# A depthwise convolution moved from diagonal matrices and VectorE onto quarter-width matmuls over shifted copies

## The chip, the cores and the metric

The kernel runs on one core of a Trainium2 chip. The core has TensorE (matmuls, PE in the profile), VectorE (DVE), ScalarE (ACT), GpSimd (POOL) and SyncE (SP), and 16 DMA engines that all queues share. The metric is device time in microseconds (us) for one execution, smaller is better.

## What is computed

The reference is a two-layer transformer for 256 positions of width 1024, in f32. Layer 0 is differential attention and a dense feed-forward part. Layer 1 is a conformer convolution and a mixture of 8 experts with 2 chosen for each position. Each layer ends with a gated embedding. The change touches the convolution of layer 1 and the start of the second expert job:

```python
def conformer_conv(h, w_pw1, b_pw1, w_dw, b_dw, ln_g, ln_b, w_pw2, b_pw2):
    u = h @ w_pw1 + b_pw1
    a, g = jnp.split(u, 2, axis=-1)
    u = a * jax.nn.sigmoid(g)
    u = lax.conv_general_dilated(u, w_dw[:, None, :], window_strides=(1,),
        padding=[(CONV_WIDTH - 1, 0)], feature_group_count=D_MODEL, ...) + b_dw
    u = jax.nn.silu(layer_norm(u, ln_g, ln_b))
    return u @ w_pw2 + b_pw2

def moe_swiglu(h, w_router, b_router, w_gate, w_up, w_down):
    ...
    for e in range(N_EXPERTS):
        out = out + gates[..., e:e + 1] * swiglu(h, w_gate[e], w_up[e], w_down[e])
```

CONV_WIDTH is 31 and the convolution is depthwise: every one of the 1024 channels has 31 taps of its own, and output position s is the sum over k of tap k times input position s - 30 + k.

## The kernel before, in words

**Weights.** SyncE streams all weights through a ring of 14 slots (`weight_ring`), one piece of 1 MB in each slot, in the order in which they are used. A piece holds two units of 128x1024. For a dense unit ScalarE rounds the raw weights to `weight_hi` (L1159), VectorE subtracts to get `weight_lo` (L1614, in the second expert job L2203) and TensorE multiplies three times (L516 to L518); the two have four buffers each. `lo_done` counts the units whose raw data is no longer needed, and SyncE's `load` (L381) waits on it before it refills a slot. Everything on SyncE is in one order, so that whatever it waits for holds back all loads behind it.

**The convolution stage.** `U_PW1` (16 units) is the first projection of the convolution, `U_PW2` (8 units) the second, `U_MOE` the first expert's first unit. The projection puts channels in the partitions, in eight blocks of 128 channels. It makes blocks 0 to 3 first (8 units), then blocks 4 to 7. After each half `glu_scale` (L1893, L1895), the sigmoids on ScalarE (L1382) and `glu` (L1904) leave `conv_in_T`, eight blocks with 30 zeros and then 256 positions. `glu_done` is 1 when blocks 0 to 3 are there and 2 when all are.

- TensorE does blocks 0 to 3 (`PE_BLOCKS`). For each tap ScalarE scales the identity by the 128 channels' tap (L1393, `diagonals`), and TensorE multiplies this diagonal with the shifted input (L785): 31 matmuls of 256 columns in f32 for each block. ScalarE empties the bank and adds the bias (L1401).
- VectorE does blocks 4 to 7 (`DVE_BLOCKS`): for each block one multiplication with bias (L1924) and 30 multiply-adds (L1928).

Then comes the layer norm: a matmul with ones for the mean (L795, eight blocks), centring (L1935), squares (L1417), a matmul with ones for the variance (L799), root, reciprocal, scaling, silu, and the second projection.

**The experts.** VectorE works out a table of jobs. Job 0 is a light one (64 rows or fewer, raw f32 weights, `light_job`, matmuls L866 and L875), job 1 a big one (`big_job`: the expert with most rows, hi/lo matmuls L516 to L518 for 128 rows and quarter-width f32 matmuls for 32 rows more, L1008), then pairs of a light and a small job, then light ones. At the start of `big_job` TensorE waits for `selg_done`, which VectorE raises when the gated one-hot of the job is made (`one_hot_gated`, L2034); on VectorE this comes behind the four additions of job 0's result (`scatter_add`, L2146). The one-hot is first read by the transposes behind the fourth unit (`in_gate`, i == 3).

GpSimd loads two rows that are spread over all partitions: the bias of the second projection once the first scaled pair of the layer norm is there (`cn_done`, L501), which VectorE adds to the residual (L1949), and the norm's gains later (L504).

Of the kernel before, what the change touches and what calls it, by code (L numbers as in the profile page):

```python
# [38 lines left out]
def program(nc, x, p, mix_norm_g, ffn_norm_g, attn_w_qkv, attn_w_o, attn_g_q, attn_g_k,  # L39
# [52 lines left out]
    with ExitStack() as ctx:  # L92
        def sb(name, shape, dt=F32, to=ctx):
            return to.enter_context(nc.sbuf_tensor(name, shape, dt))
# [23 lines left out]
        taps, mask, upper, wr, wr2, lamv = overlay(  # L118
            ("conv_taps", [P, TAPS * KT], F32), ("causal_mask", [P, P], F32), ("strict_upper", [P, P], F32),
            ("router_raw", [P, KT, NE], F32), ("router_hi_lo", [P, KT, 2 * NE], F32R),  # L120
            ("lambda_vectors", [P, 4, HD], F32))
        xel, sgl, hTl, selTl = overlay(
# [36 lines left out]

        cT, cy, csq = overlay(("conv_in_T", [P, KT, TAPS - 1 + S], F32), ("conv_out_T", [P, KT, S], F32),  # L160
                              ("conv_square", [P, KT, S], F32))
# [5 lines left out]
        _, pnat = overlay(("before_p_rows", [P, 5 * D], F32), ("p_rows", [P, T, 2 * P], F32))  # L167
        sb("stage_region", [P, KT * (TAPS - 1 + S) + 2 * KT * S])
        NDIAG = 8

        def diag(n):

            at = CW + n % 4 * P
            return xn[:, n % NDIAG // 4, at:at + P]

# [17 lines left out]
        NV = 91  # L193
        TAPROWS = TAPS * KT // 2
        stage_v = kT[0:NV, 0, 0:P]
        stage_t = [kT[0:TAPROWS, 1, 0:P], kT[0:TAPROWS, 2, 0:P]]

# [65 lines left out]
        glu_done = sem("glu_done")  # L263
        diag_done = sem("diag_done")
        diag_used = sem("diag_used")
        convp_done = sem("convp_done")
        conv_done = sem("conv_done")
        mean_ready = sem("mean_ready")
# [104 lines left out]
        def _(sp):  # L373
# [14 lines left out]
            def feed_forward(first, wg, wu, wd, j=None, proj=None):  # L388
# [44 lines left out]
            tap_rows = conv_w_dw[0].rearrange("k (c n) -> (k c) n", n=P)  # L433
            for i in range(2):
                sp.dma_start(stage_t[i], tap_rows[i * TAPROWS:(i + 1) * TAPROWS, :]).then_inc(consts_in, 16)
            sp.wait_ge(consts_in, 16 * N_CONSTS)
# [73 lines left out]
        def _(pe):  # L510
# [78 lines left out]
            def feed_forward(u0, n0, j, job, side, gap=0):  # L589

                u = u0
                for s in range(STEPS):
# [18 lines left out]
                    for i in range(4):  # L611
# [7 lines left out]

            pe.wait_ge(consts_in, 16 * N_CONSTS)  # L620
            pe.wait_ge(masks_done, 4)
            pe.transpose(ps[:, 0, 0:NV], stage_v, ident[0:NV, 0:NV])
            pe.transpose(ps[:, 0, P:P + TAPROWS], stage_t[0], ident[0:TAPROWS, 0:TAPROWS])
            pe.transpose(ps[:, 0, 2 * P:2 * P + TAPROWS], stage_t[1],
                         ident[0:TAPROWS, 0:TAPROWS]).then_inc(vecsT_ready, 1)

# [152 lines left out]

            n = 0  # L780
            pe.wait_ge(glu_done, 1)
            for ch in PE_BLOCKS:
                for k in range(TAPS):
                    pe.wait_ge(diag_done, n + 1)
                    pe.matmul(ps[:, 4 + ch, 0:S], diag(n), cT[:, ch, k:k + S],  # L785
                              start=k == 0, stop=k == TAPS - 1).then_inc(diag_used, 1)
                    n += 1

            pe.wait_ge(glu_done, 2)
            for n, ch in enumerate(PE_BLOCKS + DVE_BLOCKS):  # L790
                if ch in PE_BLOCKS:
                    pe.wait_ge(convp_done, PE_BLOCKS.index(ch) + 1)
                else:
                    pe.wait_ge(conv_done, DVE_BLOCKS.index(ch) + 1)
                last = pe.matmul(ps[:, 0, 0:S], ones[:, :], cy[:, ch, :], start=n == 0, stop=n == KT - 1)  # L795
            last.then_inc(mean_ready, 1)
# [185 lines left out]
            def big_job(j):  # L982
# [89 lines left out]
                def in_gate(s):  # L1072

                    def behind(i):
# [78 lines left out]
        def _(act):  # L1153
# [231 lines left out]

            def diagonals(first, n):

                for m in range(first, n):
                    i, k = m // TAPS, m % TAPS
                    if m >= NDIAG:  # L1390
                        act.wait_ge(diag_used, m - NDIAG + 1)
                    at = k * KT + PE_BLOCKS[i]
                    act.activation(diag(m), ident[:, :], ACT.Copy, scale=taps[:, at:at + 1]).then_inc(diag_done, 1)  # L1393
                    if i and k == 4:
                        conv_out(i - 1)

            def conv_out(i):

                ch = PE_BLOCKS[i]
                act.wait_ge(diag_used, TAPS * (i + 1))  # L1400
                act.activation(cy[:, ch, :], ps[:, 4 + ch, 0:S], ACT.Identity,  # L1401
                               bias=vecs[:, V_BDW + ch:V_BDW + ch + 1]).then_inc(convp_done, 1)

            split.to(U_PW1 + 7 + 4)
            sigmoids(0)
            diagonals(0, NDIAG)
            split.to(U_PW1 + 15 + 4)
            diagonals(NDIAG, NDIAG + 4)
            sigmoids(1)
            split.to(U_PW2 + 4)  # L1410
            diagonals(NDIAG + 4, TAPS * len(PE_BLOCKS))
            conv_out(len(PE_BLOCKS) - 1)
            act.wait_ge(mean_ready, 1)
# [197 lines left out]
        def _(dve):  # L1611
# [45 lines left out]


            dve.memset(eps, EPS)
            own.step(dve.memset(lneps, LN_EPS))  # L1660
# [7 lines left out]
            for t in range(T):  # L1668
# [3 lines left out]
            dve.tensor_copy(vecs[:, 0:NV], ps[:, 0, 0:NV])  # L1672
            own.step(dve.tensor_copy(taps[:, :].rearrange("p (a n) -> p a n", a=2),
                                     ps[:, 0, P:3 * P].rearrange("p (a n) -> p a n", a=2)[:, :, 0:TAPROWS]))
            own.step(dve.tensor_scalar(gsub, vecs[:, V_GSUB:V_GSUB + 1], 1.0 - LAM0, None, ALU.mult))
# [209 lines left out]
            own.wait(n)  # L1885
            dve.sem_inc(rdiag_done, 1)
            own.step(dve.memset(cT[:, :, 0:TAPS - 1], 0.0))

# [30 lines left out]
            last_of = {}  # L1919
            for k in range(TAPS):  # L1920
                for ch in DVE_BLOCKS:
                    src, w = cT[:, ch, k:k + S], taps[:, k * KT + ch:k * KT + ch + 1]
                    if k == 0:
                        last_of[ch] = own.add(dve.tensor_scalar(  # L1924
                            cy[:, ch, :], src, w, vecs[:, V_BDW + ch:V_BDW + ch + 1], ALU.mult, ALU.add))
                        continue
                    own.wait(last_of[ch])
                    ins = dve.scalar_tensor_tensor(cy[:, ch, :], src, w, cy[:, ch, :], ALU.mult, ALU.add)  # L1928
                    if k < TAPS - 1:
                        last_of[ch] = own.add(ins)  # L1930
                    else:
                        ins.then_inc(conv_done, 1)
            dve.wait_ge(mean_done, 1)
# [394 lines left out]
```

## Time and profile before

| | us |
|---|---|
| median of 3 runs (1554.34 to 1562.11) | 1556.78 |
| the profiled execution, its own time | 1555.64 |
| its span, first to last instruction | 1553.9 |
| TensorE busy in the span | 1447.0 (93%) |
| VectorE busy | 770.5 (50%) |
| ScalarE busy | 665.9 (43%) |
| DMA, mean rate over the span | 285 GB/s |

The span is what the rows of the trace add up to. The profiled execution took 1.74 us more than its span, and the median of the runs lies 1.14 us above it. The busy shares are averages over stages with different limits. An f32 matmul has two records in the trace, so that L785 with 124 matmuls stands there as x248, and L1008 with 32 matmuls in a section as x64; an fp32r matmul (L516 to L518) has one.

### The profile page before, as it was taken

To read this page: it belongs to the slowest core of one execution; us is meant where nothing else is said; L and a number is where in the kernel's file an instruction comes from. 1 tells how busy PE (TensorE), PEld (TensorE's weight loads), DVE (VectorE), ACT (ScalarE), POOL (GpSimd) and SP (SyncE) were. 2 spreads that over 40 slices of the span, in tenths; PEclk is the share of its full clock that TensorE was granted. 3 is DMA by queue.
4 is the path that set the end of the run, shared out by engine and by line. 5 is a ranking of instruction groups with operands and counts; after the bars stand their busy time and mean duration, and the time that the engine had idled before them with its cause. 6 is when DMAs were issued, how large, how long until landed. Compare 5 with 4: busy or idle time off the path is not lost.

```text
span 1553.9 us, 19566 instructions
## 1 busy us (share of the span) xinstructions
PE 1447.0 (93%) x7460; PEld 987.9 (64%) x7460; DVE 770.5 (50%) x1029; ACT 665.9 (43%) x955; POOL 9.1 (1%) x23
## 2 busy tenths in 40 slices
PE   6988999999889977989999999999899999998777
PEld 5866788887789865337777534887335887342236
DVE  5665554455666956025676301988104897000016
ACT  4575544444556742014565201777004775000014
POOL 1000000000000000000000000000000000000000
PEclk9988999999999986998999999999999999999999
DMA  9923555555444022998768699999999999999991
GB/s 312 362 93 104 177 178 189 185 190 189 136 163 136 1 82 75 413 406 351 287 255 324 220 413 406 412 408 410 357 406 412 413 408 410 410 406 412 413 401 63
DMA packets 131334, 442.43 MB, mean 285 GB/s; under 512 B 7059, under 2 KB 7398, under 8 KB 118966
## 3 DMA queue, kind: packets, MB, share of 16 engines
q1 hardware_dynamic: 130144, 438.46, 73.7%
q0 software_dynamic: 928, 2.79, 0.6%
q8 instruction: 58, 0.95, 0.2%
q14 instruction: 22, 0.18, 0.0%
q10 hardware_dynamic: 182, 0.05, 0.0%
HBM read 440.22 MB, written 1.05 MB: 284 GB/s over the span
## 4 chain that ended last, share of the span: by engine, by line
PE 79%; DMA 10%; DVE 4%; ACT 2%; issue 2%; SPq 2%; ACTq 0%; DVEq 0%
PE psum L516 17%; PE psum L518 17%; PE psum L517 17%; PE psum L866 15%; DMA weight_ring<-in_moe_w_down 4%; DMA weight_ring<-in_moe_w_gate 4%; PE psum L785 3%; SPq L381 2%; DMA weight_ring<-in_moe_w_up 2%; PE psum L1008 1%; PE psum L831 1%; PE psum L829 1%; PE psum L1022 1%; DVE weight_lo L1614 1%; PE psum L541 1%
## 5 line engine op out<-in xcount | busy, mean ns | idle before, releaser
L1159 ACT ACTIVATE weight_hi<-weight_ring 128x1024 fp32r<-128x1024 f32 x412 | 431.0, 1059 | 257.8 <-PE psum L518 252.9
L1614 DVE TENSOR_TENSOR weight_lo<-weight_ring,weight_hi 128x1024 fp32r<-128x1024 f32 x328 | 393.9, 1223 | 176.5 <-ACT weight_hi L1159 170.8
L866 PE MATMUL psum<-weight_ring,silu_gate 128*64 128x512 f32 x960 | 219.8, 608 | 13.3 <-DMA weight_ring<-in_moe_w_up 5.6
L516 PE MATMUL psum<-weight_hi,act_hi 128*128 128x512 f32 x448 | 180.2, 402 | 11.6 <-issue 5.6
L517 PE MATMUL psum<-weight_lo,act_hi 128*128 128x512 f32 x448 | 178.3, 398 | 0.0
L518 PE MATMUL psum<-weight_hi,act_lo 128*128 128x512 f32 x448 | 178.1, 398 | 0.0
L2159 DVE TENSOR_TENSOR hidden<-silu_gate,psum 128x512 f32<-128x512 f32 (+1 forms) x20 | 12.4, 622 | 332.7 <-PE psum L866 296.7
L866 PEld LDWEIGHTS psum<-weight_ring,silu_gate 128*64 128x64 f32 x960 | 67.2, 139 | 153.0 <-issue 130.9
L516 PE MATMUL psum<-weight_hi,job_act_hi 128*128 128x512 f32 x336 | 136.3, 406 | 5.4 <-issue 4.9
L866 PE MATMUL psum<-weight_ring,hidden_T 128*64 128x512 f32 x560 | 128.5, 598 | 12.7 <-DMA weight_ring<-in_moe_w_down 12.6
L517 PE MATMUL psum<-weight_lo,job_act_hi 128*128 128x512 f32 x336 | 133.8, 398 | 0.0
L518 PE MATMUL psum<-weight_hi,job_act_lo 128*128 128x512 f32 x336 | 133.8, 398 | 0.0
L2203 DVE TENSOR_TENSOR weight_lo<-weight_ring,weight_hi 128x1024 fp32r<-128x1024 f32 x84 | 101.8, 1224 | 48.6 <-ACT weight_hi L1159 46.1
L1471 ACT ACTIVATE hidden_T<-psum 128x512 f32<-128x512 f32 (+1 forms) x20 | 10.9, 544 | 244.9 <-PE psum L891 244.9
L516 PE MATMUL psum<-weight_hi,hidden_T_hi 128*128 128x512 f32 x280 | 111.0, 397 | 0.0
L518 PE MATMUL psum<-weight_hi,hidden_T_lo 128*128 128x512 f32 x280 | 110.6, 395 | 0.0
L517 PE MATMUL psum<-weight_lo,hidden_T_hi 128*128 128x512 f32 x280 | 110.6, 395 | 0.0
L516 PEld LDWEIGHTS psum<-weight_hi,act_hi 128*128 128x128 f32 x448 | 85.4, 191 | 32.0 <-issue 10.0
L866 PEld LDWEIGHTS psum<-weight_ring,hidden_T 128*64 128x64 f32 x560 | 37.9, 136 | 95.4 <-issue 66.5
L518 PEld LDWEIGHTS psum<-weight_hi,act_lo 128*128 128x128 f32 x448 | 85.3, 190 | 20.2
L517 PEld LDWEIGHTS psum<-weight_lo,act_hi 128*128 128x128 f32 x448 | 85.5, 191 | 19.3
L516 PEld LDWEIGHTS psum<-weight_hi,job_act_hi 128*128 128x128 f32 x336 | 64.0, 191 | 25.8 <-issue 8.4
(336 smaller groups left out, 1645.8 us busy)
## 6 DMA issues: line engine op xcount, KB each, us to landing
weight_ring<-in_moe_w_gate SPq DMA_DIRECT2D x112, 1024.0 KB, 18.3
weight_ring<-in_moe_w_up SPq DMA_DIRECT2D x112, 1024.0 KB, 18.1
weight_ring<-in_moe_w_down SPq DMA_DIRECT2D x112, 1024.0 KB, 16.0
weight_ring<-in_ffn_w_gate SPq DMA_DIRECT2D x14, 1024.0 KB, 5.2
weight_ring<-in_ffn_w_up SPq DMA_DIRECT2D x14, 1024.0 KB, 5.1
weight_ring<-in_ffn_w_down SPq DMA_DIRECT2D x14, 1024.0 KB, 5.1
weight_ring<-in_attn_w_qkv SPq DMA_DIRECT2D x12, 1024.0 KB, 14.3
weight_ring<-in_conv_w_pw SPq DMA_DIRECT2D x12, 1024.0 KB, 5.1
```

Of the source, the lines that this page charges most:

```text
L381: sp.dma_start(dst, src).then_inc(piece_in[slot], 16)
L516: pe.matmul(dst, ahi_, bhi_, start=first, stop=False, **kw)
L517: pe.matmul(dst, ahi_, blo_, start=False, stop=False, **kw)
L518: return pe.matmul(dst, alo_, bhi_, start=False, stop=last, **kw)
L541: last = pe.transpose(ps[:, bank, at:at + P], src[:, t, kt * P:(kt + 1) * P], ident[:, :])
L785: pe.matmul(ps[:, 4 + ch, 0:S], diag(n), cT[:, ch, k:k + S], start=k == 0, stop=k == TAPS - 1).then_inc(diag_used, 1)
L829: pe.matmul(ps[:, bank, k * P:(k + 1) * P], hhi[:, t, cols], sel[:, t, :], start=t == 0, stop=False)
L831: last = pe.matmul(ps[:, bank, k * P:(k + 1) * P], hlo[:, t, cols], sel[:, t, :], start=False, stop=t == T - 1)
L866: ins = pe.matmul(ps[halves[half], bank, :], lhs, raw(u)[:, half * CW:(half + 1) * CW], start=first, stop=last)
L1159: act.activation(whi[:, u % SPLIT, :], raw(u), ACT.Copy).then_inc(hi_done, 1)
L1614: dve.tensor_tensor(wlo[:, u % SPLIT, :], raw(u), whi[:, u % SPLIT, :].bitcast(F32), ALU.subtract).then_inc(lo_done, 1)
L2203: dve.tensor_tensor(wlo[:, (U_MOE + u) % SPLIT, :], raw(U_MOE + u), whi[:, (U_MOE + u) % SPLIT, :].bitcast(F32), ALU.subtract).then_inc(bi ...
```

## The change

All eight blocks go to TensorE. A block's 128 channels are four groups of 32 (g). For each block and group, SyncE copies the group's 32 partitions of `conv_in_T` to the four quarters of the partitions of a new buffer `x4`, quarter c shifted by c positions. A matmul then contracts over 128 rows = 4 taps x 32 channels: 8 steps k of 4 taps each (32 taps, the last one zero), output 32 channels in a quarter of the bank, 256 columns. That is 8 x 8 x 4 = 256 matmuls of 128x32 weights. VectorE makes the weights, 128 x 1024 for a block (`tap_weights`), from the stacked identity `ident4` and the taps; blocks 0 to 3 between the splits of the second half of the projection, 4 to 7 behind `glu(1)`, each of these when the block four before it is done.

The copies are 48 DMAs: 16 with blocks 0 to 3 after `glu_done` 1, and 16 each with blocks 4, 5 and with blocks 6, 7 after `glu_done` 2. `x4` and the weights lie in seven slots of the weight ring (pieces 2 to 8 of the first expert); so SyncE makes the copies after the expert's first two pieces and loads the next one only when `conv4_used` is 8, that is when the convolution is finished. At the start the taps come in 8 DMAs of 128-byte runs in place of 2 (18 constants in place of 12), and VectorE makes `ident4` before it raises `vecs_done`.

The diagonals on ScalarE and the taps on VectorE are gone. `big_job` waits for `selg_done` ahead of the transposes and no longer at its start.

```diff
-N_CONSTS = 12
+N_CONSTS = 18
...
-PE_BLOCKS = [0, 1, 2, 3]
-DVE_BLOCKS = [4, 5, 6, 7]
+TAPG = 8
+CG = 32
...
+        X4_PIECE = U_MOE // 2 + 2
+        X4W = 4 * (TAPG - 1) + S
...
+            def shifted_copies():
+                for part, blocks in enumerate((slice(0, 4), slice(4, 6), slice(6, 8))):
+                    cc = (part + 1) // 2
+                    sp.wait_ge(lo_done, U_PW1 + 6 + 4 * cc)
+                    sp.wait_ge(glu_done, cc + 1)
+                    for g in range(4):
+                        for c in range(4):
+                            n = min(X4W, TAPS + S - c)
+                            sp.dma_start(x4[c * CG:(c + 1) * CG, blocks, g, 0:n],
+                                         cT[g * CG:(g + 1) * CG, blocks, c:c + n]).then_inc(x4_in[part], 16)
+                sp.wait_ge(conv4_used, KT)
...
+                        if j is None and unit == 0 and i == X4_PIECE - U_MOE // 2:
+                            shifted_copies()
...
-            for ch in PE_BLOCKS:
-                for k in range(TAPS):
-                    pe.wait_ge(diag_done, n + 1)
-                    pe.matmul(ps[:, 4 + ch, 0:S], diag(n), cT[:, ch, k:k + S],
-                              start=k == 0, stop=k == TAPS - 1).then_inc(diag_used, 1)
+            for ch in range(KT):
+                pe.wait_ge(x4_in[max(ch // 2 - 1, 0)], 16 * 16)
+                pe.wait_ge(w4_done, ch + 1)
+                if ch >= 4:
+                    pe.wait_ge(convp_done, ch - 3)
+                for k in range(TAPG):
+                    for g in range(4):
+                        rows = slice(g * CG, (g + 1) * CG)
+                        last = pe.matmul(ps[rows, 4 + ch % 4, 0:S], w4(ch)[:, k, rows],
+                                         x4[:, ch, g, 4 * k:4 * k + S], start=k == 0, stop=k == TAPG - 1)
+                last.then_inc(conv4_used, 1)
...
                         if s == 0 and i == 3:
                             pe.wait_ge(sc_done, 4 * j + 4)
+                            pe.wait_ge(selg_done, j + 1)
...
-                pe.wait_ge(selg_done, j + 1)
...
+            own.step(dve.reduce_sum(ident4[:, :], ident[:, :].rearrange("p (c n) -> p n c", n=CG), AX))
...
+            def tap_weights(b):
+                if b >= 4:
+                    dve.wait_ge(conv4_used, b - 3)
+                dve.tensor_tensor(w4(b).rearrange("p k (g n) -> p (k g) n", n=CG),
+                                  ident4[:, :].unsqueeze(1).broadcast_to([P, 4 * TAPG, CG]),
+                                  taps[:, b * 4 * TAPG:(b + 1) * 4 * TAPG].unsqueeze(2)
+                                  .broadcast_to([P, 4 * TAPG, CG]), ALU.mult).then_inc(w4_done, 1)
+
+            for b in range(4):
+                split.to(U_PW1 + 13 + 2 * b)
+                dve.wait_ge(lo_done, U_PW1 + 10 + 2 * ((b + 1) // 2))
+                tap_weights(b)
```

## Rows read from the trace of the kernel before

**Rows 1.** The chain that ended last around the convolution: start, length, what.
```profile
462.54 1.23 DVE conv_square L1893
...
488.09 53.69 PE psum L785 x248
...
543.54 2.01 PE psum L795 x8
545.57 0.39 ACT normed L1414
```

**Rows 2.** VectorE in order of time, in and behind the projection's second half.
```profile
465.54 1.67 DVE L1904 SCALAR_TENSOR_TENSOR conv_in_T<-conv_square,column_vectors 128x256 f32<-128x256 f32 x4 [0.64 <-ACT conv_square L1382]
...
486.43 1.23 DVE L1614 TENSOR_TENSOR weight_lo<-weight_ring,weight_hi 128x1024 fp32r<-128x1024 f32 x1 [1.62 <-ACT weight_hi L1159]
...
493.97 1.67 DVE L1904 SCALAR_TENSOR_TENSOR conv_in_T<-conv_square,column_vectors 128x256 f32<-128x256 f32 x4
...
497.08 47.59 DVE L1928 SCALAR_TENSOR_TENSOR conv_out_T<-conv_in_T,conv_taps,conv_out_T 128x256 f32<-128x256 f32 x120
```

**Rows 3.** A section of 32 quarter-width f32 matmuls in the chain of the big job.
```profile
721.46 3.59 PE psum L1008 x64
```

**Rows 4.** SyncE's weight loads from 425 to 500 us: issue ns min/median/max; landing.
```profile
L381 SPq DMA_DIRECT2D weight_ring<-in_moe_w_gate x7: 367/368/368, 430.1 to 494.1; - x7
...
DMA to landing us min/median/max: 4.9/5.1/5.4
```

**Rows 5.** The first microseconds in order of time: DMA issues and the first matmul.
```profile
0.80 0.86 SPq L432 DMA_DIRECT2D residual<-in_x  x2
...
1.71 0.72 SPq L435 DMA_DIRECT2D k_T<-in_conv_w_dw  x2
...
4.77 0.28 ACTq L1173 DMA_DIRECT2D k_T<-in_attn_g_sub  x1
...
9.45 0.41 PE L622 MATMUL psum<-identity,k_T 91*128 91x91 f32 x1 [9.45 <-DMA k_T<-in_attn_g_sub]
```

**Rows 6.** Stretches: length, busy us (count) of each engine, granted clock, DMA share, GB/s.
```profile
545.60:548.30 2.70, 0.00 (x0) 0.00 (x0) 2.31 (x2) 1.41 (x2) 0.00 (x0) 1.00 0.00 0
548.30:554.00 5.70, 5.41 (x16) 4.14 (x16) 0.05 (x1) 2.54 (x4) 0.00 (x0) 0.70 0.00 0
...
695.10:700.00 4.90, 0.00 (x1) 0.02 (x1) 4.90 (x9) 0.04 (x1) 0.00 (x0) 0.92 1.02 408
700.00:709.00 9.00, 8.99 (x37) 8.42 (x37) 1.64 (x3) 1.06 (x1) 0.00 (x0) 0.50 1.03 410
```

**Rows 7.** Longer stretches of the expert jobs, same columns.
```profile
608.00:660.00 52.00, 51.53 (x229) 17.28 (x231) 5.57 (x19) 5.03 (x8) 0.00 (x0) 0.94 0.91 361
...
738.00:777.00 39.00, 39.00 (x300) 28.87 (x291) 25.27 (x23) 22.38 (x24) 0.00 (x0) 1.00 0.74 287
...
1204.00:1515.00 311.00, 286.11 (x1371) 154.92 (x1370) 110.13 (x112) 98.95 (x113) 0.03 (x1) 1.00 1.03 409
```

**Rows 8.** The chain that ended last at the start of the big job.
```profile
693.12 1.99 PE psum L920 x8
695.10 4.90 issue
700.01 0.77 PE psum L516
...
712.72 0.38 PE psum L517
```

**Rows 9.** VectorE at the start of the big job.
```profile
696.91 2.48 DVE L2146 TENSOR_TENSOR residual<-residual,psum 128x512 f32<-128x512 f32 x4
699.30 0.60 DVE L2034 TENSOR_SCALAR one_hot_gated<-iota,job_positions,job_gates 128x128 f32<-128x128 f32 x2
```

**Rows 10.** The bias row: GpSimd's issue, and VectorE's use of it.
```profile
557.09 0.76 POOL L501 DMA_DIRECT2D conv_in_T<-in_conv_b_pw  x1 [410.23 <-DVE conv_out_T L1940]
...
564.15 2.35 DVE L1949 TENSOR_TENSOR residual<-residual,conv_in_T 128x1024 f32<-128x1024 f32 x2
```

More of the change, by code:

```diff
@@ L116, in overlay @@
                 return [sb(name, shape, dt, phase) for name, shape, dt in specs]
-        taps, mask, upper, wr, wr2, lamv = overlay(
-            ("conv_taps", [P, TAPS * KT], F32), ("causal_mask", [P, P], F32), ("strict_upper", [P, P], F32),
+        taps, mask, upper, wr, wr2, lamv, ident4 = overlay(
+            ("conv_taps", [P, KT * TAPG * 4], F32), ("causal_mask", [P, P], F32), ("strict_upper", [P, P], F32),
             ("router_raw", [P, KT, NE], F32), ("router_hi_lo", [P, KT, 2 * NE], F32R),
-            ("lambda_vectors", [P, 4, HD], F32))
+            ("lambda_vectors", [P, 4, HD], F32), ("stacked_identity", [P, CG], F32))
         xel, sgl, hTl, selTl = overlay(
@@ L167, in program, with w4 @@
         _, pnat = overlay(("before_p_rows", [P, 5 * D], F32), ("p_rows", [P, T, 2 * P], F32))
[L168 to L174, printed above, removed]
+        sb("stage_region", [P, KT * (TAPS + S) + 2 * KT * S])
+        X4_PIECE = U_MOE // 2 + 2
+        X4W = 4 * (TAPG - 1) + S
+        X4_SLOT = X4_PIECE % RING
+        assert X4_SLOT + 7 <= RING
+        shared = ring[:, X4_SLOT:X4_SLOT + 7, :].rearrange("p s n -> p (s n)")
+        x4 = shared[:, 0:KT * 4 * X4W].rearrange("p (b g n) -> p b g n", b=KT, g=4)
+        W4_AT = KT * 4 * X4W
+        def w4(b):
+            at = W4_AT + b % 4 * TAPG * P
+            return shared[:, at:at + TAPG * P].rearrange("p (k n) -> p k n", k=TAPG)
         ps = ctx.enter_context(nc.psum_tensor("psum", [P, 8, CW], F32))
@@ L263, in program @@
         glu_done = sem("glu_done")
-        diag_done = sem("diag_done")
-        diag_used = sem("diag_used")
+        tap_pad_done = sem("tap_pad_done")
+        x4_in = [sem(f"shifted_in{i}") for i in range(3)]
+        w4_done = sem("tap_weights_done")
+        conv4_used = sem("conv_block_done")
         convp_done = sem("convp_done")
-        conv_done = sem("conv_done")
         mean_ready = sem("mean_ready")
@@ L778, in _ @@
                     last.then_inc(rbc_ready, 1)
-            n = 0
-            pe.wait_ge(glu_done, 1)
-            for ch in PE_BLOCKS:
-                for k in range(TAPS):
-                    pe.wait_ge(diag_done, n + 1)
-                    pe.matmul(ps[:, 4 + ch, 0:S], diag(n), cT[:, ch, k:k + S],
-                              start=k == 0, stop=k == TAPS - 1).then_inc(diag_used, 1)
-                    n += 1
-            pe.wait_ge(glu_done, 2)
[L790 to L795, printed above, removed]
+            for ch in range(KT):
[3 more added lines that the diff above has]
+                    pe.wait_ge(convp_done, ch - 3)
+                for k in range(TAPG):
+                    for g in range(4):
[3 more added lines that the diff above has]
+                last.then_inc(conv4_used, 1)
+            pe.wait_ge(glu_done, 2)
+            for ch in range(KT):
+                pe.wait_ge(convp_done, ch + 1)
+                last = pe.matmul(ps[:, 0, 0:S], ones[:, :], cy[:, ch, :], start=ch == 0, stop=ch == KT - 1)
             last.then_inc(mean_ready, 1)
@@ L1384, in sigmoids, with conv_out @@
                 ins.then_inc(glu_sig, 1)
[L1386 to L1401, printed above, removed]
+            def conv_out(ch):
+                act.wait_ge(conv4_used, ch + 1)
+                act.activation(cy[:, ch, :], ps[:, 4 + ch % 4, 0:S], ACT.Identity,
                                bias=vecs[:, V_BDW + ch:V_BDW + ch + 1]).then_inc(convp_done, 1)
@@ L1405, in _ @@
             sigmoids(0)
-            diagonals(0, NDIAG)
             split.to(U_PW1 + 15 + 4)
-            diagonals(NDIAG, NDIAG + 4)
             sigmoids(1)
             split.to(U_PW2 + 4)
-            diagonals(NDIAG + 4, TAPS * len(PE_BLOCKS))
-            conv_out(len(PE_BLOCKS) - 1)
+            for ch in range(KT):
+                conv_out(ch)
             act.wait_ge(mean_ready, 1)
@@ L1672, in _ @@
             dve.tensor_copy(vecs[:, 0:NV], ps[:, 0, 0:NV])
-            own.step(dve.tensor_copy(taps[:, :].rearrange("p (a n) -> p a n", a=2),
-                                     ps[:, 0, P:3 * P].rearrange("p (a n) -> p a n", a=2)[:, :, 0:TAPROWS]))
+            dve.tensor_copy(taps[:, :].rearrange("p (b k g) -> p k b g", k=TAPG, g=4),
+                            ps[:, 0, P:3 * P].rearrange("p (k b g) -> p k b g", k=TAPG, g=4))
+            own.step(dve.reduce_sum(ident4[:, :], ident[:, :].rearrange("p (c n) -> p n c", n=CG), AX))
             own.step(dve.tensor_scalar(gsub, vecs[:, V_GSUB:V_GSUB + 1], 1.0 - LAM0, None, ALU.mult))
@@ L1917, in _ @@
             glu(1)
[L1919 to L1932, printed above, removed]
+            for b in range(4, KT):
+                tap_weights(b)
             dve.wait_ge(mean_done, 1)
```

21 lines of the change are left out of this document (12 added, 9 removed).

## The prediction

> **What bounds the kernel now.** I read the page first (93% of the span TensorE is busy, which says nothing of single stages), then the chain that ended last, then the order of time around each edit, and last the table by stretches.
>
> In the chain the convolution is one piece. TensorE's diagonals take 53.7 us for 124 matmuls and the matmuls for the mean end at 545.5 [rows 1]. The reader is to see that two engines end together here: VectorE's 120 multiply-adds run from 497.08 to 544.67 [rows 2]. Taking over one half alone would leave the other half as the bound. The change takes over both, so the whole stretch from the projection's end (TensorE free at about 487.7, 0.4 before the chain's 488.09) to 545.5 is at stake.
>
> At the start of the big job the chain has 4.9 us in which TensorE does nothing, and after it matmuls of 0.43 us (1.2 GHz: 512 columns) until 713.1 [rows 8]. In that time VectorE adds the light job's result and makes the one-hot, which ends at 699.9 [rows 9]. The granted clock is 0.50 in the 9 us behind the idle time [rows 6].
>
> Behind that the stretches say which resource sets the pace [rows 7]. In the big job TensorE is busy all the time at full clock and the DMA moves 287 GB/s: TensorE sets it. At the end of the kernel the DMA runs at 409 GB/s, and DMA sets it. SyncE is then held by the full ring and not by the DMA, so a shift of TensorE's work ahead of them shifts the later DMA stream too, and a gain is handed on.
>
> **The change part by part.** All times are on the span of the profiled execution (1553.9).
>
> *Matmuls of the convolution.* The nearest row has the same form, 128x32 f32 weights and 256 columns, four quarters in turn: 32 of them take 3.59 us [rows 3], 0.112 each. A diagonal took 53.69/124 = 0.433 [rows 1]. 256 x 0.112 = 28.7 us, 3.6 for a block, against 53.7. Blocks 0 to 3: 487.7 to 502.1.
>
> *VectorE's taps* (124 instructions, 49 us) go. It gets 8 products of 128x1024 at 1.23 each, as L1893 for as many [rows 1]. The first four lie between splits, where VectorE waits 1.62 for each unit [rows 2]. The fourth starts at 487.7 and ends at 488.9, and `glu_scale(1)` starts 0.8 later. I cost this at nothing: ScalarE no longer makes four diagonals ahead of the sigmoids, which gives the time back. So `glu(1)` ends as before at 493.97 + 1.67 = 495.6 [rows 2]. Weights 4 to 7 are made behind it, by 503.3 at the latest, ahead of their blocks. ScalarE's 124 diagonals go too; their time lay beside TensorE's.
>
> *Copies.* This is new and the trace has no copy within the core. Each part is 16 DMAs, of 145 KB in the first (32 partitions x 4 blocks x 1136 bytes) and 73 KB in the others. The issue: between 0.37 us [rows 4] and 0.46 (two loads of x and then the taps start 0.91 apart) [rows 5]. I take 0.40, near the middle. The landing: a 1 MB load lands 5.1 after its issue [rows 4] and moves in 1.05 MB / 409 GB/s = 2.56 [rows 7], so 2.5 is fixed; the other end is 4.6, from the last constant's issue to the first matmul [rows 5]. I take 3.0, nearer the first row, as it is the same queue.
> - Part 0: the sources are ready at 465.54 + 1.67 = 467.2; 16 x 0.40 + 3 gives 477. Even at twice this it is before 487.7: hidden behind the second half of the projection.
> - Part 1: 495.8 + 15 x 0.40 + 3.0 = 504.8. TensorE has been free since 502.1, so 2.7 us idle are left.
> - Part 2: 495.8 + 31 x 0.40 + 3.0 = 511.2.
>
> *The end.* An idle time of 2.7 us at 545.6 was followed by a clock of 0.70 over 5.7 us [rows 6], which there cost 5.41 - 8 x 0.433 = 1.9 us. I add 1.5. Blocks 4, 5: 504.8 + 7.2 + 1.5 = 513.5, later than part 2. Blocks 6, 7: 520.7. The mean: seven of its matmuls run while ScalarE empties the last bank, 8 x 0.433 = 3.5: 524.1. Before 545.5: **gain 21.4**. Ends of this term: 25.7 if no copy is waited for (487.7 + 28.7 + 3.5 = 519.9), and what the slow rivals below give.
>
> *What SyncE holds back.* Behind `conv4_used` the loads of 12 pieces wait, among them the first expert's. Two are in the ring; ten more start at 520.7 instead of during the projection and take 10 x 2.56 + 2.5 = 28 us, to 549. The light job starts at 608, where the first stretch begins [rows 7], then at 587. Slack 38 us: cost nothing. Without that cover each late microsecond would cost one. The bias row is issued at 557.09 and first used at 564.15 [rows 10]; now it shares the engines with these loads. VectorE can wait some 3 us for it and splits ahead of need by about as much. I take nothing; the other end is 3 us.
>
> *Start.* SyncE issues eight DMAs for taps from 1.71 [rows 5]: the last at 1.71 + 7 x 0.40 = 4.5, beside ScalarE's last at 4.77, and all loads wait for all constants. 992 runs of 128 bytes are new; between 0 and 2 us, I take 0.2, as the last issue is no later. The sum that makes `ident4` is priced at the 128x128 operation of VectorE, 0.3 [rows 9], on the path. **Loss 0.5.**
>
> *The wait in the big job.* The same wait comes behind three more units. Until then TensorE has unit 0, 32 gather matmuls and units 1 to 3, so VectorE's one-hot at 699.9 is no longer waited for [rows 9]. The 4.9 idle go [rows 8]. The work from 700.0 to 713.1 was at half clock, at full it takes 6.5. Nothing excludes either end: 4.9 (clock down anyway) and 11.4. The gather has 32 columns per matmul, and 6.7 us of it did not bring the clock up [rows 6]; whether it keeps it up is open. I take the middle, a clock that falls once behind the gather: **gain 8.4**. It is handed on, since TensorE paces the big job [rows 7].
>
> Sum: 1553.9 - 21.4 + 0.5 - 8.4 = 1524.6. The profiled execution took 1.7 more than its span and the median lies 1.1 above: **1527.5**.
>
> *A rule against it.* The fixed part of a load overlaps with other loads, since 1 MB pieces stream at 409 GB/s though each lands 5.1 after its issue [rows 4, 7]. The Trainium skill (DMA: Bandwidth & Descriptors, section Anatomy of one DMA) gives 2.0 us plus bytes over 436 GB/s for a DMA, and its rules for kernel authors tell one to coalesce transfers. Taken one behind another, 48 copies would by that page take an estimated 107 us and the kernel would end near 1590; taken as overlapping, the page leaves the sum as it is.
>
> **The rivals.**
> - *Copies twice as slow* (0.8 us each, by issue or by their 1136-byte runs). Against: a 1 MB load is issued in 0.37. For: no copy from SBUF to SBUF is in the trace, and 32 partitions at a time may not use what 128 do. Part 2 lands at 495.8 + 24.8 + 3 = 523.6, the mean ends at 523.6 + 7.2 + 1.5 + 3.5 = 535.8, the gain is 9.7: total 1539.
> - *The big job gives less*: half clock all along (4.9: total 1531), or the DMA paces its start, as it moves 410 GB/s there [rows 6], and all is lost: 1536.
> - *Better*: the copies are never waited for and the clock holds: 1553.9 - 25.7 - 11.4 + 0.3 + 2.8 = 1520.
> - *Other side: the copies run one after another.* Each costs its fixed 2.5 and 0.2 of moving; 48 end at 467.3 + 130 = 597, the mean ends at 609, 64 later: total 1612, slower. It decides from 1.37 us a copy on, where part 2 lands at 541.2 and the convolution loses as much as the big job gives. For it: nothing but that these are small and many. Against: the streaming loads.
> - *No net effect of the first part*: the convolution's time comes back while the light job waits for its pieces, total 1549. It would need the loads 38 us later than worked out, and speaks against itself by that.
>
> **How the numbers follow.** Forecast 0.55 (1523 to 1532 by its own bounds), slow copies 0.17, the big job gives less 0.13, better 0.05, one after another or another wait of that size 0.05, no net effect 0.05. Range 1517 to 1541: it takes in all but the last two. 0.5% is 7.8 us, about what a measurement of this kernel can tell from no change. Faster than 1549: 0.90, same 0.05, slower 0.05.
>
> **What would show it.** The convolution's matmuls become 512 records with 0.11 us per matmul. SyncE has 48 issues 0.4 apart, from 467 and from 496. TensorE idles about 3 us after the fourth block and none after the sixth. VectorE has eight 1.23 us products. The mean ends near 524, the light job starts near 587 with its first pieces in the ring. The big job's first matmul follows the last L920 at once. The prediction is wrong if the copies are further apart than 0.8, if the first weight load starts later than 11 us, or if the light job waits for its first pieces.

## The result, and the profile after

| | median us (runs) | beside it, before | ratio, 95% interval |
|---|---|---|---|
| changed kernel | 1534.03 (1532.50 to 1540.33, 4) | 1558.17 (4) | 0.9861 [0.9835, 0.9887] |

24 us faster by the medians and 22 by the ratio; forecast were 1527.5 and a gain of 29. The profiled execution took 1533.46 with a span of 1531.7, which is 22.2 under the span before; the sum in the forecast gave 1524.6. The two traces cut at the same five places, with the rows of before from the same views:

| stretch | before | after | difference |
|---|---|---|---|
| start to the mean's end | 545.5 | 530.95 | -14.6 |
| to the light job's first matmul | 63.2 | 65.0 | +1.8 |
| light job, to the matmuls that scatter it | 84.4 | 85.8 | +1.4 |
| to the first quarter-width matmul of the big job | 28.3 | 17.3 | -11.0 |
| to the span's end | 832.5 | 832.7 | +0.2 |

Lines have moved: L812 are the convolution's matmuls, L819 the mean (L795 before), L423 the copies, L387 `load`, L540 to L542 the hi/lo matmuls (L516 to L518), L944 the scatter (L920), L1032 the quarter-width section (L1008).

TensorE of the changed kernel in order of time (start, length; in brackets idle time and what ended it):

```profile
489.60 14.02 PE L812 MATMUL psum<-weight_ring 128*32 128x256 f32 x256
508.86 9.02 PE L812 MATMUL psum<-weight_ring 128*32 128x256 f32 x128 [5.24 <-DMA weight_ring<-conv_in_T]
520.19 7.11 PE L812 MATMUL psum<-weight_ring 128*32 128x256 f32 x128 [2.31 <-DMA weight_ring<-conv_in_T]
```

The reader is to see two idle times that a DMA ends, where the forecast had one, of 2.7. 256 records are 128 matmuls, so one takes 0.110. This replaces the L785 piece of [rows 1].

The issues in the changed kernel's view of L423, and the chain that ended last at the end of the copies:

```profile
L423 SPq DMA_DIRECT2D weight_ring<-conv_in_T x48: 585/597/1659, 467.5 to 518.1; - x48
...
DMA to landing us min/median/max: 2.0/2.1/3.9
```

```profile
495.45 1.59 DVE conv_in_T L1917 x4
497.17 0.58 SPq L423
497.80 0.60 SPq L423
...
510.00 1.66 SPq L423
...
517.45 0.60 SPq L423
518.09 2.06 DMA weight_ring<-conv_in_T
520.19 7.11 PE psum L812 x128
527.30 3.67 PE psum L819 x16
```

SyncE's queue is now on the chain: 32 issues, one each 0.64 us but for one of 1.66, from 497.17 to 518.1. Only the last copy's landing stands behind them. The issue of a weight load took 0.367 in [rows 4].

Stretches of the changed kernel (length; busy us (count) of PE, PEld, DVE, ACT, POOL; granted clock; DMA share; GB/s):

```profile
465.20:468.70 3.50, 3.49 (x17) 3.49 (x18) 2.84 (x5) 1.43 (x3) 0.00 (x0) 0.54 0.00 0
467.50:478.00 10.50, 10.50 (x86) 10.50 (x86) 6.19 (x6) 3.18 (x3) 0.00 (x0) 0.96 0.78 173
497.00:507.50 10.50, 6.62 (x124) 3.74 (x116) 4.84 (x5) 1.21 (x3) 0.00 (x0) 0.93 0.42 100
...
509.00:518.00 9.00, 8.88 (x128) 4.32 (x125) 0.00 (x0) 0.51 (x2) 0.00 (x0) 0.79 0.42 100
...
683.70:688.60 4.90, 4.90 (x40) 4.63 (x38) 4.90 (x9) 1.14 (x2) 0.00 (x0) 1.00 1.02 407
688.60:693.50 4.90, 4.90 (x25) 4.06 (x26) 3.44 (x5) 2.70 (x4) 0.00 (x0) 1.00 1.02 408
```

While the second half is copied, the DMA engines are busy for 0.42 of the time: the wait is for issues and not for bytes. In the last two rows TensorE is busy all along at the full clock, where [rows 6] had 4.9 us idle and then 0.50.

### The profile page after: what moved, and what is told of

It is laid out like the page before. It is cut to its first block, busy times and chain, and to the rows that moved or that the text cites. A ratio compares the mean times of both kernels' runs of the same rounds, so it can differ in the third digit from the quotient of the medians.

```text
span 1531.7 us, 19925 instructions
## 1 busy us (share of the span) xinstructions
PE 1418.7 (93%) x7724; PEld 953.9 (62%) x7724; DVE 730.9 (48%) x916; ACT 624.1 (41%) x835; POOL 9.1 (1%) x23
## 4 chain that ended last, share of the span: by engine, by line
PE 78%; DMA 10%; DVE 5%; SPq 2%; ACT 2%; issue 2%; DVEq 0%; ACTq 0%
PE psum L540 17%; PE psum L542 17%; PE psum L541 17%; PE psum L890 16%; DMA weight_ring<-in_moe_w_down 5%; DMA weight_ring<-in_moe_w_gate 4%; DMA weight_ring<-in_moe_w_up 2%; PE psum L1032 1%; SPq L423 1%; PE psum L855 1%; PE psum L853 1%; SPq L387 1%; DVE weight_lo L1624 1%; PE psum L1046 1%; PE psum L565 1%
## 5 line engine op out<-in xcount | busy, mean ns | idle before, releaser
L540 PE MATMUL psum<-weight_hi,act_hi 128*128 128x512 f32 x448 | 181.2, 405 | 11.6 <-issue 5.6
L542 PE MATMUL psum<-weight_hi,act_lo 128*128 128x512 f32 x448 | 178.9, 399 | 0.0
L2172 DVE TENSOR_TENSOR hidden<-silu_gate,psum 128x512 f32<-128x512 f32 (+1 forms) x20 | 12.4, 620 | 332.2 <-PE psum L890 296.0
L540 PE MATMUL psum<-weight_hi,job_act_hi 128*128 128x512 f32 x336 | 134.9, 402 | 0.5 <-DVE weight_lo L1624 0.5
L542 PE MATMUL psum<-weight_hi,job_act_lo 128*128 128x512 f32 x336 | 132.7, 395 | 0.0
L540 PE MATMUL psum<-weight_hi,hidden_T_hi 128*128 128x512 f32 x280 | 111.0, 396 | 0.0
L542 PE MATMUL psum<-weight_hi,hidden_T_lo 128*128 128x512 f32 x280 | 110.6, 395 | 0.0
L540 PEld LDWEIGHTS psum<-weight_hi,act_hi 128*128 128x128 f32 x448 | 86.0, 192 | 32.3 <-issue 10.0
L542 PEld LDWEIGHTS psum<-weight_hi,act_lo 128*128 128x128 f32 x448 | 85.7, 191 | 20.5
L540 PEld LDWEIGHTS psum<-weight_hi,job_act_hi 128*128 128x128 f32 x336 | 63.3, 188 | 20.6 <-issue 3.4
## 6 DMA issues: line engine op xcount, KB each, us to landing
weight_ring<-in_attn_w_qkv SPq DMA_DIRECT2D x12, 1024.0 KB, 14.3
```

Of the source, the lines that this page charges most:

```text
L540: pe.matmul(dst, ahi_, bhi_, start=first, stop=False, **kw)
L542: return pe.matmul(dst, alo_, bhi_, start=False, stop=last, **kw)
```

## The experiments

All were timed beside the kernel before; those with one run have no interval.

**One edit at a time.** The kernel before with the moved wait alone:

```diff
                             pe.wait_ge(sc_done, 4 * j + 4)
+                            pe.wait_ge(selg_done, j + 1)
...
-                pe.wait_ge(selg_done, j + 1)
```

> The kernel before with nothing but the moved wait for the gated one-hot. Theory: TensorE starts the big job about 4.9 us sooner, its clock never falls, so that its 13 us of work at half clock take 6.5, and since TensorE paces the big job all 11.0 us are handed on: some 1547 us against 1558. Rival (the DMA paces the start of the big job): TensorE stalls for weights a little later and the kernel stays at 1558. Rival (clock falls anyway): 1553.

Measured 1551.61 (7 runs, 1545.78 to 1552.48), 0.9953 [0.9936, 0.9969]. Two stretches of its trace, at the big job's start:

```profile
695.10:699.00 3.90, 3.90 (x30) 3.59 (x29) 3.90 (x6) 1.21 (x2) 0.00 (x0) 1.00 1.03 406
...
700.00:705.00 5.00, 5.00 (x15) 4.13 (x16) 1.69 (x5) 1.10 (x2) 0.00 (x0) 0.50 1.03 410
```

The idle 4.9 us are gone, and the clock falls once, behind the gather. From the first scatter matmul to the first quarter-width one it takes 20.4 us against 28.3: 7.8 gained, near the forecast's 8.4; the ratio makes it 7.3 of 1558, and the two medians lie 5.7 apart. The theory's clock that never falls did not come true here. The changed kernel itself shows 17.3, gain 11.0, as its clock does not fall. Over the ten traces of kernels with this edit this stretch has only these two values, 17.3 in four and 20.4 or 20.5 in six; kernels with the same big job lie on either side.

The changed kernel with the wait put back where it was, so the convolution alone:

> The changed kernel with the wait put back to the start of the big job. Theory: the two parts of the change add up, so this kernel is 11 us above the changed one, at 1545, and the convolution alone is worth 12 to 13 us. Rival (the convolution's gain is partly the same time as that of the wait, through the DMA stream): the sum of the two parts alone differs from the whole by 3 us or more.

Measured 1541.85 (4 runs), 0.9887 [0.9864, 0.9911]. The two parts are 0.47% and 1.13%, together 1.60% against 1.39% for the whole. The 3.3 us between them would be enough for the rival, but the intervals reach 3 to 4 us to either side, so the parts add up as far as these runs can tell. Its big job takes 28.2 from scatter to quarter-width matmuls, as before.

**The copies.** The second half in one portion of 16 copies, each twice as large:

```diff
-                for part, blocks in enumerate((slice(0, 4), slice(4, 6), slice(6, 8))):
-                    cc = (part + 1) // 2
+                for part, blocks in enumerate((slice(0, 4), slice(4, 8))):
+                    cc = part
...
-                pe.wait_ge(x4_in[max(ch // 2 - 1, 0)], 16 * 16)
+                pe.wait_ge(x4_in[ch // 4], 16 * 16)
```

> The second half copied in one portion: 16 copies of 142 KB in place of 32 of 71 KB. Theory (a copy costs SyncE 0.64 us whatever it holds): the portion is there at about 510.3, against 508.9 and 520.2 for the two, TensorE does blocks 4 to 7 without a second gap, the convolution ends near 525.5 in place of 527.3, gain 1 to 2 us. Rival (the bytes set the pace, 1.28 us for twice the bytes): the portion is there at 520, the convolution ends at 535 and the kernel loses 7 us.

Measured 1536.11 (4 runs), 0.9856 [0.9834, 0.9879]: no difference to the changed kernel. SyncE and TensorE in order of time:

```profile
496.69 11.25 SPq L423 DMA_DIRECT2D weight_ring<-conv_in_T  x16
```

```profile
510.65 16.31 PE L812 MATMUL psum<-weight_ring 128*32 128x256 f32 x256 [7.48 <-DMA weight_ring<-conv_in_T]
```

16 copies of 142 KB were issued in 11.25 us, 0.6 to 0.7 each, as 71 KB ones are. Between 71 and 142 KB a copy's price does not hang on its bytes. With two portions TensorE begins block 4 earlier (508.86 against 510.65) and has to stop once more, and the mean starts at 526.89 against 527.23: the gain of 1 to 2 us that was expected isn't there.

Half of the second half's copies (groups 2 and 3) issued by ScalarE beside SyncE's:

```diff
-                    for g in range(4):
+                    for g in (range(4) if cc == 0 else range(0, 2)):
...
-            for ch in range(KT):
-                conv_out(ch)
+            act.wait_ge(lo_done, U_PW1 + 10)
+            act.wait_ge(glu_done, 2)
+            for part, blocks in ((1, slice(4, 6)), (2, slice(6, 8))):
+                for g in range(2, 4):
+                    for c in range(4):
+                        act.dma_start(...).then_inc(x4_in[part], 16)
+                for ch in (range(4) if part == 1 else range(4, KT)):
+                    conv_out(ch)
```

> The copies of groups 2 and 3 of the second half are issued by ScalarE's queue, beside SyncE's of groups 0 and 1. Theory (the issue on one queue is the limit): both portions take half the time, the first is there at about 504, the second at 511, TensorE ends the convolution near 520 in place of 527.3, gain 6 to 8 us. Rival (descriptor making is shared by the queues, or the DMA engines are the limit for copies of 32 partitions): the copies stay 0.64 us apart over both queues together and nothing is gained.

Measured 1527.61 (4 runs), 0.9794 [0.9766, 0.9822]. The two queues, then TensorE:

```profile
499.40 11.49 SPq L423 DMA_DIRECT2D weight_ring<-conv_in_T  x16
```

```profile
499.40 5.46 ACTq L1427 DMA_DIRECT2D weight_ring<-conv_in_T  x8
```

```profile
506.87 14.26 PE L812 MATMUL psum<-weight_ring 128*32 128x256 f32 x256 [1.03 <-DMA weight_ring<-conv_in_T]
521.06 3.72 PE L819 MATMUL psum<-conv_out_T,ones 128*128 128x256 f32 x16
```

ScalarE's 16 copies are issued beside SyncE's at nearly the same price (median 0.64 against 0.60), and all 32 begin within 12.5 us in place of 20.9, so most of the cost is each engine's own and not something they share. The mean starts at 521.06, although the first copy of the second half was issued 2.2 us later in this run. The ratio is 0.7% under that of the changed kernel. The Trainium skill (DMA: Bandwidth & Descriptors, Rules for kernel authors) says that spreading DMAs over issuing engines does not help bandwidth, as they share the same DMA engines, and only saves issue time. The trace agrees: with one queue the DMA engines were busy for 0.42 of the time and moved 100 GB/s, so issue time was what was short, and in the next kernel the two queues together moved 177.

The same with the second half's inputs earlier:

```diff
-            for b in range(4):
+            for b in range(3):
                 split.to(U_PW1 + 13 + 2 * b)
...
                 tap_weights(b)
             split.to(U_PW1 + 15 + 4)
             glu_scale(1)
-            split.to(U_PW2 + 4)
+            dve.wait_ge(lo_done, U_PW1 + 14)
+            tap_weights(3)
             glu(1)
+            split.to(U_PW2 + 4)
```

> The two queues, and on VectorE glu_scale(1) ahead of the fourth block's tap weights and glu(1) ahead of the split of the last unit. Theory (the chain is glu, issue, landing, matmuls): glu(1) ends about 3 us sooner, TensorE's gap closes further, total gain against the changed kernel 9 to 11 us: some 1524. Rival (TensorE is already the limit with two queues): no more than the two queues alone.

Measured 1527.53 (5 runs), 0.9806 [0.9786, 0.9827]. TensorE, then the stretch of the copies:

```profile
487.55 21.18 PE L812 MATMUL psum<-weight_ring 128*32 128x256 f32 x384
509.56 7.12 PE L812 MATMUL psum<-weight_ring 128*32 128x256 f32 x128 [0.84 <-DMA weight_ring<-conv_in_T]
516.61 3.72 PE L819 MATMUL psum<-conv_out_T,ones 128*128 128x256 f32 x16
```

```profile
497.00:507.00 10.00, 9.96 (x188) 5.75 (x180) 2.45 (x2) 1.68 (x4) 0.00 (x0) 1.00 0.69 177
```

Blocks 0 to 5 run without a gap and 0.84 us are left before 6 and 7. The mean starts 4.5 earlier than with two queues alone, but the median is the same. The rival of this run holds: TensorE was already the limit. The projection, whose matmuls are the same in all these kernels, happened to come to its last matmul at 487.34 in this trace and at 491.61 in the one with two queues, and that is 4.3 of the 4.5. That matmul in the kernel before, the changed one, with two queues, and with early inputs:

```profile
487.81 0.28 PE L518 MATMUL psum<-act_hi,weight_lo 128*128 128x256 f32 x1
489.39 0.28 PE L542 MATMUL psum<-act_hi,weight_lo 128*128 128x256 f32 x1
491.61 0.28 PE L542 MATMUL psum<-act_hi,weight_lo 128*128 128x256 f32 x1
487.34 0.28 PE L542 MATMUL psum<-act_hi,weight_lo 128*128 128x256 f32 x1
```

Measured from its start (us; the last row is the kernel without second copies, below):

| kernel | to the end of `glu(1)` | to the mean's first matmul |
|---|---|---|
| changed | 7.64 | 37.84 |
| one portion | 7.62 | 37.95 |
| two queues | 7.65 | 29.45 |
| two queues, early inputs | 5.66 | 29.27 |
| no second copies | 7.64 | 27.97 |

So the second queue gains 8.4 us, and inputs that are 2.0 earlier another 0.2.

The big job starts 5.5 earlier in this trace; from the first quarter-width matmul to the span's end it then takes 836.8, against 834.1. That stretch, the same code, took 832.5 to 837.1 over the eleven traces with these jobs. Some 3 of these 4.6 us are the clock. In the five traces where it fell behind the gather it falls again 156 us further on, behind an idle time of 2.0 us that all have; to one instruction shortly behind it these five take 165.1 or 165.2, the other six 163.5. And in four traces, this one among them, it falls once more some 801 us in; from one instruction 777 to 780 us in to the end these four take 57.2 to 57.4, the others 55.7 or 55.8. What is left is open.

The bound: no second copies at all, blocks 4 to 7 read those of blocks 0 to 3, which changes the data behind it and with them the experts' jobs. Only the convolution can be compared.

```diff
-                for part, blocks in enumerate((slice(0, 4), slice(4, 6), slice(6, 8))):
+                for part, blocks in enumerate((slice(0, 4),)):
...
-                                         x4[:, ch, g, 4 * k:4 * k + S], ...)
+                                         x4[:, ch % 4, g, 4 * k:4 * k + S], ...)
```

> The changed kernel without the 32 copies of blocks 4 to 7; their matmuls read the copies of blocks 0 to 3, so this part of the result is left out. Theory (the issue of the copies on SyncE sets the end of the convolution): TensorE runs 8 blocks without a gap, 28.8 us from about 488 to 489.6 on, the convolution ends near 518 in place of 527.3 and the kernel gains 8 to 10 us: some 1525. Rival (weights from VectorE or the emptying of banks hold the second half too): under 4 us, with waits of TensorE for VectorE or ScalarE in the trace.

Its whole time was 1641.17 (4 runs), with other jobs. Its convolution:

```profile
488.04 27.83 PE L812 MATMUL psum<-weight_ring 128*32 128x256 f32 x512
515.80 3.72 PE L819 MATMUL psum<-conv_out_T,ones 128*128 128x256 f32 x16
```

27.83 for 256 matmuls, 28.7 in the forecast. The mean starts 11.4 us before the changed kernel's (527.23 - 515.80), of which 1.6 are the changed kernel's later projection. So the second half's copies, together with the wait for their inputs, which this kernel leaves out too, cost 9.9 us (37.84 - 27.97), and with two queues 1.5 are left.

**What an issue costs.** 15 additional copies while SyncE has nothing else to do, three of each kind: within the core 32 partitions x 4 runs of 1136 bytes (L423), 4 runs of 1024 (L425), one run of 4544 (L427), 128 partitions x 1136 (L429), and from HBM 32 x 4 x 1136 (L431).

```diff
+                sp.wait_ge(lo_done, U_PW1 + 6)
+                for i in range(3):
+                    sp.dma_start(runs[i][0:CG, :, 0:X4W], four[0:CG, :, 0:X4W]).then_inc(probe_in, 16)
...
+                sp.wait_ge(probe_in, 15 * 16)
```

> A look at what the issue of a copy depends on. Before the first portion of copies SyncE issues fifteen more DMAs into the ring slots that the portion overwrites, three of each form: 32 partitions x 4 runs of 1136 bytes within SBUF (the change's form), 32 x 4 x 1024 bytes within SBUF, 32 x 1 run of 4544 bytes within SBUF, 128 partitions x 1 run of 1136 bytes within SBUF, and 32 x 4 x 1136 bytes from HBM. Theory (the number of runs in a partition, not bytes or partitions, sets it): the two-dimensional forms take about 0.4 us, the three-dimensional ones 0.6, whatever the source. Rival (SBUF as the source sets it): all four SBUF forms take 0.6 and the one from HBM 0.4. Rival (the 1136-byte run): 1024-byte runs take less.

Measured 1529.16 (1 run). Issues in ns, min/median/max:

```profile
L423 SPq DMA_DIRECT2D weight_ring<-residual x3: 587/613/759, 448.1 to 449.5; - x3
```

```profile
L427 SPq DMA_DIRECT2D weight_ring<-residual x3: 588/598/607, 452.1 to 453.4; - x3
```

```profile
L431 SPq DMA_DIRECT2D weight_ring<-in_conv_w_pw x3: 597/617/650, 456.8 to 458.2; - x3
```

All five kinds had a median of 0.60 to 0.62: none of the three theories holds. So a second probe: within the core, each issued when the one before it has landed (L423); from HBM, 128 partitions x 1136 bytes, spaced likewise (L426) and one behind another (L429).

```diff
+                    sp.dma_start(runs[i][0:CG, :, 0:X4W], four[0:CG, :, 0:X4W]).then_inc(probe_in, 16)
+                    sp.wait_ge(probe_in, 16 * i + 16)
```

> The probe before this one found 0.60 us per issue in every form, where three or more copies stood behind one another. It is taken up again at the same place (SyncE idle for want of work), in three groups of three: (a) copies within the core, 32 partitions x 4 runs of 1136 bytes, each issued only when the one before it has landed; (b) copies from HBM, 128 partitions x 1 run of 1136 bytes, spaced in the same way; (c) the same from HBM one behind another. Theory 'place': an issue costs 0.37 when the queue is empty and 0.60 when it is issued behind another. Then (a) and (b) are 0.37 to 0.40 for all three and (c) is 0.4 for the first and 0.60 for the rest. Theory 'kind': a copy within the core costs 0.60 and one from HBM with a run per partition 0.37. Then (a) is 0.60, (b) and (c) are 0.37. Theory 'run length': what made the weight loads cheap is their 4096-byte runs. Then all nine are 0.60. The kernel's time stays within 1 us of the changed kernel's but for what the spaced copies hold back on SyncE (some 20 us, ahead of the first shifted copies and inside their idle time of 30): 1527 to 1538.

Measured 1536.32 (1 run).

```profile
L423 SPq DMA_DIRECT2D weight_ring<-residual x3: 585/586/763, 448.2 to 453.3; - x3
```

```profile
L426 SPq DMA_DIRECT2D weight_ring<-in_conv_w_pw x3: 328/352/353, 456.3 to 461.2; - x3
```

```profile
L429 SPq DMA_DIRECT2D weight_ring<-in_conv_w_pw x3: 328/431/433, 463.7 to 464.5; - x3
```

With one run in each of 128 partitions the kind decides: within the core an issue is 0.60 (L429 of the first probe), from HBM 0.35. Within the core it is 0.59 even into an empty queue. Standing in line adds 0.08 to the one from HBM. A store from SBUF to HBM took 0.34 (L492 of the changed kernel), so it is not the source in SBUF alone. But from HBM in 32 x 4 runs it is 0.62 (L431), so the shape can cost as much as the kind. Whether it is the 32 partitions or the 4 runs there, and why neither adds to a copy within the core, wasn't tried. Both probes ran once.

**Loads held back.** The next loads wait, besides `conv4_used`, for the first scaled pair of the layer norm (`cn_done`), or for the router's scores (`log_ready`):

```diff
                 sp.wait_ge(conv4_used, KT)
+                sp.wait_ge(cn_done, 1)
```

> SyncE holds the first expert's remaining loads until the first scaled pair of the layer norm, about 15 us longer than the change does. Theory (the held-back loads have 40 us of slack before the light job): no difference within 1.5 us. Rival (part of the convolution's gain is lost to the held loads): 10 to 15 us slower.

> SyncE holds the same loads until the router's logits, at about 580, some 52 us longer than the change does. Theory (DMA paces the light job once the ring is empty, so loads that start later than about 568 cost one for one): piece 15 of the expert starts 11 us later than in the changed kernel, which becomes 8 to 13 us at the end. Rival (the light job has slack in its weights): no difference.

Measured 1533.02 (4 runs), 0.9836 [0.9809, 0.9864], and 1547.41 (5 runs), 0.9932 [0.9909, 0.9956]. The first load after the copies, in the one and in the other:

```profile
543.59 0.89 SPq L387 DMA_DIRECT2D weight_ring<-in_moe_w_gate  x2
```

```profile
580.61 0.89 SPq L387 DMA_DIRECT2D weight_ring<-in_moe_w_gate  x2
```

16 us later than the changed kernel (527.37) cost nothing that the median shows; 53 later cost 11 by the ratios of the two kernels and 13 by their medians, and 14 or 15 against the kernel with the shorter delay; the forecast's slack of 38 leaves 15. In the trace 9.4 of it are in the light job, which takes 95.2 in place of 85.8, as from 643 on it waits some 0.6 for nearly every piece. 3.2 more are the big job's clock, which fell in this trace, and 4.5 the last stretch, in which it fell two times more than in the changed kernel's, as told above. So what the lateness alone costs lies between 9.4 and 15.

## Why the prediction was right, and by which step it was off

- *One term was mis-sized: the issue of a copy*, "I take 0.40", bounds 0.37 and 0.46. It measured 0.64, and 0.675 on the average over the 32 copies. From the first issue to the last it took 20.9 us and not 12.4, so part 2 landed at 520.2, not 511.2, and the next sentence, blocks 4 and 5 end "later than part 2", fell. The 9.0 are 8.5 for the issues and 1.4 for a later `glu(1)`, less 0.9 for the landing; 2.3 of them were hidden behind blocks 4 and 5. The mean ended at 530.95 in place of 524.1, gain 14.6 in place of 21.4. The bounds came from loads from HBM with one or two runs per partition; 0.64 lies between them and the 0.8 of the rival "by issue", nearer the rival. Given that the trace had no copy within the core, those rows bounded nothing.
- *The landing*, 3.0 from bounds 2.5 and 4.6, was 2.1 and gave back 0.9. The Trainium skill's fixed 2.0 us (DMA: Bandwidth & Descriptors, Anatomy of one DMA) is close to it, though the page has it for DMAs issued from GpSimd and these are SyncE's, which the forecast did not say; that the copies overlap, as argued in the prediction, is shown by issues 0.64 apart, each landing 2 or 3 us later.
- *`glu(1)` at 495.6* came at 497.03, and all of it is the projection, whose last matmul began at 489.39 in place of 487.81. From there to the end of `glu(1)` it is 7.6 us, against 7.8 before: the fourth block's weights, costed at nothing, cost nothing. The projection ran with a clock of 0.54 from 465.2 to 468.7 where before it was 1.00; the idle time ahead was alike, 2.6. Over all twelve traces its last matmul began between 487.3 and 491.8, at 487.8 or earlier in the three where the clock did not fall there, and in the kernel with the moved wait alone, whose code up to there is that of before, it fell too, so it does not take the new convolution to make it fall.
- *Matmuls* 0.110 for 0.112, *blocks 6, 7* 7.11 for 7.2, *the mean* 3.7 for 3.5: as forecast. *Clock behind the idle time*: 9.02 - 7.11 = 1.9 for 1.5, and it costs nothing, as part 2 is waited for anyway.
- *Loads held back, cost nothing*: right, shown by the two delays above. The bias row used its slack up: it is 7.6 us on its way and VectorE waits 0.44 for it. Between the mean and the light job 1.8 were lost, where the second projection and what follows it ran at a clock of 0.73 against 0.78. Kernels with the changed convolution took 61.5 to 65.2 there, 63.2 with the wait put back and 61.5 with one portion, against 63.2 before, so the new convolution does not set it. In the light job 1.4 went: it waits some 0.5 for each piece from 664 on, 68 us into the job, where before that began 72 us in. It took 84.0 and 84.4 with the old convolution and 84.5 to 86.0 with the new one, but for the run whose loads were held back longest. What sets those 4 us wasn't separated.
- *Start* 0.25 for 0.5: the first matmul is at 9.63 for 9.45, the first of L540 at 19.07 for 18.82.
- *The moved wait* 11.0 for 8.4 in this execution. In six of ten traces it is 7.8; both lie within the bounds 4.9 and 11.4. The forecast's picture, a clock that falls once behind the gather, is what those six show. That this execution gained 2.6 more, more than a third of what the mean lost, is luck.
- *Handed on*: the stretch behind it is the same to 0.2. In the traces where the clock fell behind the gather some 1.7 of the gain are lost again at its next fall.

By the spans: the mean ended 6.9 later than forecast, less the 0.5 of start loss that the forecast had beside it; 3.2 were lost on the way to and in the light job, 2.6 more gained by the wait, 0.2 lost behind it. 6.9 - 0.5 + 3.2 - 2.6 + 0.2 = 7.2, and 1531.7 is 7.1 above 1524.6.

## What to carry to other kernels

When a change puts many small DMAs on one queue, work out the issues before the bytes, and take the price from a DMA of the same kind (both ends, runs per partition); if the trace has none, the ranges must go well beyond the nearest rows. If the issues are the bound, give half of them to a second engine that is idle there: this was worth 8.4 us at the mean (0.5%) and 0.7% by the ratio, more than cutting the same data otherwise (nothing). Measure a gain at its stage, since a median with 2 to 5 us of scatter cannot show one of 4, and count from an event just ahead of the edit: the projection's last matmul alone moved by 4.5 us from trace to trace, which in one run looked like the gain that was sought. Then look at the clock before calling a difference in the same code unexplained.

## What the runs showed of the hardware

- A copy within the core is issued in 0.59 to 0.60 us and the next 0.64 later, be it 71 or 142 KB, 32 or 128 partitions, 1 or 4 runs (medians; single ones take 0.8 to 1.9); alone it is 0.59 too. From HBM with a run in each of 128 partitions 0.35 alone and 0.43 in line. From HBM in 32 x 4 runs 0.62. Store to HBM 0.34. A copy within the core lands 2.1 us after its issue with 71 KB and 3.0 with 142 KB (medians; 2.0 to 3.9).
- The queues of SyncE and ScalarE issue such copies side by side, 32 of them within 12.5 or 14.3 us where one queue took 20.9: 177 GB/s together where one had 100.
- 32-partition copies of 142 KB moved 173 GB/s with the DMA engines busy for 0.78 of the time, and weight loads 409 at 1.03: 173/0.78 = 222 against 409/1.03 = 397, a bit over half in the same busy time. The copies differ from the loads in partitions, in run length and in their source, and which of these it is wasn't separated.
- Four quarter-width f32 matmuls of 256 columns take 0.44 us together, and a full-width one of 128x128 0.433 [rows 1]: four taps for the price of one.
- The granted clock behind the same 32 matmuls of 32 columns is either held at 1.00 (four traces) or falls to 0.50 once (six), and which of them cannot be read from the code. In every trace where it fell, of those with the same jobs, it fell again 156 us further on, and in none of the others.
